# The last four weight tiles of a sublayer finished in four parts in place of three, in a two-layer decoder trunk

## What is computed

```python
mod = (cs @ ada_w[l] + ada_b[l])[:, None, :]
sh_a, sc_a, g_a, sh_m, sc_m, g_m = jnp.split(mod, N_MOD, axis=-1)
h = x * (1.0 + sc_a) + sh_a
y = gla_mixer(h, ...)    # layer 1: sb_mixer
x = layer_norm(DEEPNORM_ALPHA * x + (1.0 + g_a) * y, ln_g[l, 0], ln_b[l, 0])
h = x * (1.0 + sc_m) + sh_m
y = sq_relu_mlp(h, mlp_w1[l], mlp_b1[l], mlp_w2[l], mlp_b2[l])
x = layer_norm(DEEPNORM_ALPHA * x + (1.0 + g_m) * y, ln_g[l, 1], ln_b[l, 1])
```

## Time and profile before

| | |
|---|---|
| median of 3 runs | 2352.53 us (2351.28 to 2353.08) |
| profiled execution, its own time | 2352.33 us |
| its span | 2350.6 us |
| mean granted TensorE clock | 0.984 |
| TensorE busy | 2272.8 us, 97% of the span |
| Vector busy | 1748.5 us, 74% |
| Scalar busy | 1145.8 us, 49% |
| GpSimd busy | 25.8 us, 1% |

### The profile page before, as it was taken

How to read it: one execution, slowest core, us unless ns; L and a number is a source line. 1 busy time by engine, 2 the same in 40 slices (tenths; PEclk the granted TensorE clock), 3 DMA queues, 4 the chain that set the end, 5 groups by cost and what they waited for, 6 DMA issues and landing times.

```text
span 2350.6 us, 31199 instructions
## 1 busy us (share of the span) xinstructions
PE 2272.8 (97%) x10336; PEld 1869.3 (80%) x10336; DVE 1748.5 (74%) x1675; ACT 1145.8 (49%) x1383; POOL 25.8 (1%) x38
## 2 busy tenths in 40 slices
PE   5799999999999999999999999999999999999997
PEld 3578878778888888888878888887888888888886
DVE  6889688897777788898896865669765445556656
ACT  3254466364444545444455545545444455444443
POOL 1000000000000000000000000000000000000001
PEclk8899999999999999999999999999999999999998
DMA  9979888879888888879978865676776555655563
GB/s 381 385 299 366 326 322 310 317 278 345 332 317 329 324 336 336 335 259 343 346 298 300 309 237 179 243 273 239 277 282 217 190 183 179 212 191 196 192 229 117
DMA packets 145689, 653.91 MB, mean 278 GB/s; under 512 B 16400, under 2 KB 16656, under 8 KB 115520
## 3 DMA queue, kind: packets, MB, share of 16 engines
q1 hardware_dynamic: 144000, 642.05, 74.3%
q0 software_dynamic: 1600, 10.69, 1.2%
HBM read 650.57 MB, written 2.10 MB: 278 GB/s over the span
## 4 chain that ended last, share of the span: by engine, by line
PE 89%; DVE 5%; DMA 3%; issue 2%; ACT 0%; SPq 0%; DVEq 0%; ACTq 0%
PE ps L1090 28%; PE ps L1092 28%; PE ps L1091 28%; DMA R<-in_mods 2%; PE ps L1132 2%; DVE w_lo L696 1%; DMA mod_w<-in_mods 1%; DMA raw<-in_tiles 1%; PE ps L1145 1%; DVE X L761 1%; DVE S L760 1%; DVE mod_w L701 1%; DVE stats L763 1%; PE ps L1243 0%; PE ps L1259 0%
## 5 line engine op out<-in xcount | busy, mean ns | idle before, releaser
L696 DVE TENSOR_TENSOR w_lo<-raw,w_hi 128x1024 fp32r<-128x1024 f32 x768 | 935.5, 1224 | 541.3 <-ACT w_hi L330 512.2
L1090 PE MATMUL ps<-w_hi,h_hi 128*128 128x512 f32 x3072 | 1215.1, 396 | 4.0 <-DVE w_lo L696 4.0
L1092 PE MATMUL ps<-w_hi,h_lo 128*128 128x512 f32 x3072 | 1201.1, 391 | 0.0
L1091 PE MATMUL ps<-w_lo,h_hi 128*128 128x512 f32 x3072 | 1200.5, 391 | 0.0
L330 ACT ACTIVATE w_hi<-raw 128x1024 fp32r<-128x1024 f32 x768 | 810.1, 1059 | 749.4 <-PE ps L1092 681.9
L1090 PEld LDWEIGHTS ps<-w_hi,h_hi 128*128 128x128 f32 x3072 | 580.8, 189 | 131.3 <-DVE w_lo L696 12.9
L1092 PEld LDWEIGHTS ps<-w_hi,h_lo 128*128 128x128 f32 x3072 | 579.6, 189 | 122.8
L1091 PEld LDWEIGHTS ps<-w_lo,h_hi 128*128 128x128 f32 x3072 | 580.9, 189 | 118.2 <-issue 0.7
L701 DVE SCALAR_TENSOR_TENSOR mod_w<-mod_w,cs 128x2048 f32<-128x2048 f32 x200 | 457.1, 2286 | 14.1 <-ACT cs L453 7.7
L994 DVE TENSOR_TENSOR h_lo<-R,h_hi 128x512 fp32r<-128x512 f32 x128 | 87.8, 686 | 11.0 <-ACT h_hi L605 11.0
L367 ACT ACTIVATE S<-ps,b1t 128x256 f32<-128x256 f32 x128 | 50.3, 476 | 84.4 <-PE ps L1132 84.4
(11 more groups left out here) (155 smaller groups left out, 684.1 us busy)
## 6 DMA issues: line engine op xcount, KB each, us to landing
raw<-in_tiles SPq DMA_DIRECT2D x768, 512.0 KB, 4.3
mod_w<-in_mods SPq DMA_DIRECT2D x200, 1024.0 KB, 6.7
R<-in_mods SPq DMA_DIRECT2D x16, 1024.0 KB, 11.0
R<-in_ln_rows POOLq DMA_DIRECT2D x8, 1024.0 KB, 7.4
G<-in_mods SPq DMA_DIRECT2D x4, 1024.0 KB, 11.1
S<-in_mods SPq DMA_DIRECT2D x4, 1024.0 KB, 13.2
X<-in_x_rows SPq DMA_DIRECT2D x1, 2048.0 KB, 11.4
S<-in_b_rows POOLq DMA_DIRECT2D x2, 1024.0 KB, 7.2
```

The source lines that it names most:

```text
L696: nc.vector.tensor_tensor(w_lo[:, slot, :], raw[:, slot, :], w_hi[:, slot, :].bitcast(F32), ALU.subtract)\
L1090: mm(dst, hh, wh, start=start, stop=False, skip_group_check=more)
L1091: mm(dst, hh, wl, start=False, stop=False, skip_group_check=more)
L1092: return mm(dst, hl, wh, start=False, stop=stop, skip_group_check=more)
```

## The change

The first entry of LAST_PARTS, token group 0 with both banks, becomes two, one per bank. The waits on `part_done` count three raises per sublayer in place of two.

```diff
@@ -76,7 +76,7 @@
-LAST_PARTS = [(0, (0, 1)), (1, (0,)), (1, (1,))]
+LAST_PARTS = [(0, (0,)), (0, (1,)), (1, (0,)), (1, (1,))]
@@ -753,7 +753,7 @@
                 stage = S[:, tok * TW + ns[0] * SW:tok * TW + ns[0] * SW + width]
                 if half == 1 and (tok, ns) != LAST_PARTS[-1]:
-                    dve.wait_ge(part_done, 2 * occ + LAST_PARTS.index((tok, ns)) + 1)
+                    dve.wait_ge(part_done, (len(LAST_PARTS) - 1) * occ + LAST_PARTS.index((tok, ns)) + 1)
                 else:
                     dve.wait_ge(tile_used, HALF_END[occ][half])
```

## The result

The changed kernel takes 2358.59 us (median of 16 runs, 2354.03 to 2361.14), the one before 2353.59 (16 runs beside them, 2349.18 to 2357.59). The ratio is 1.0021, with a 95% interval of 1.0014 to 1.0027: about 5.0 us slower, 3.3 to 6.4. The forecast was 2.5 us slower, within 0.2%, in a range that ended at 2358.4. The direction was right, the size half of what came, and the time lies just outside the range.

A forecast was written before the change was run, and what follows sets the result against it. TensorE, busy 97% of the span, was taken to bound the kernel. Delays at three ends less the tail's gain, 1.34 + 1.04 + 1.08 - 0.99 = +2.5 us, on the 2352.53 median gave 2355.0, range 2352.8 to 2358.4.

The forecast's parts named there:

- Vector is 0.69 us late for the last product: Sublayer ends: Vector starts the last product 0.69 us after its bank is free; the split alone gains 0.7 us per end.
- Two more instructions of Vector: Each end: an extra product and update of half width, some 0.4 us, covered by TensorE's longer parts.
- TensorE's first part becomes too short for the fourth tile: Ends one to four: TensorE waits for tile four's low half; last product 1.34, 1.04, 1.08 us later, fourth level.
- The tail: After the fourth end: token 0's variance comes earlier, so GpSimd's train ends 0.99 us earlier; bounds 0.4 and 0.99.
- The rival of the held product: Fourth end: GpSimd holds Vector's last product, so the gain there falls to about 0.4 us; 2355.6 us, chance 18%.
- a fall as a rival of 22% for one and 12% for more: Clock falls in the first end's gaps, 1.7 us lost, 2356.7 (22%); at more than one end, 2358.4 (12%).
- these gaps are shorter than the 1.72 us that the clock has survived: Argument against clock falls at more than one end, the case of 2358.4 us, chance 12%.
- 0.19 + 3 x 0.23: Third end: TensorE's new gap, the old 0.19 us plus three matmuls; up to 1.9 us from the last matmul's start.
- The rival without stalls: TensorE's waits don't come: three ends gain 0.7 us each and the tail 1.6; 2348.8 us, chance 6%.
- three ends costing half of what is worked out: Reason given for the range's lower end, 2352.8 us: first three ends lose half the computed delays.

The follow-up runs named there:

- vector_only: Kernel before, TensorE keeping its three parts, Vector taking token group 0 in two pieces of 512 columns; ratio 1.0004 (0.9994 to 1.0013), 0.9 us slower.
- tensor_only: Kernel before with TensorE running the four parts, Vector taking token group 0 in one piece after the second; ratio 1.0032 (1.002 to 1.0045), 7.5 us slower.
- hooks_early_four: Changed kernel, Vector taking out the first half's columns after copies of tiles 3 and 7, not 8 and 12, in go and ao; ratio 1.0004 against before.
- late_and_mixed: Kernel before with Vector in four pieces, TensorE keeping six matmuls per tile at ends one to three, bank-by-bank order after tile one at the fourth; ratio 0.9999.
- four_at_end_four: Kernel before with the four parts at the fourth end only; ratio 0.9987 (0.9978 to 0.9996), 2350.68 against 2353.81 us.
- mixed_at_end_four: Kernel before with MIXED order and four Vector pieces at the fourth end only, transposes behind it left out; ratio 0.999, 2350.86 against 2352.48 us.

## Why the prediction was right or wrong

- **Vector is 0.69 us late for the last product**: right, and the four parts end it; in every profile with both halves of the change it starts the last product 0.48 to 0.49 us after the last matmul's start. I had used 0.43, which makes up most of the 0.07 to 0.08 us by which each end came out longer than worked out. Two more instructions of Vector, where nothing covers them, cost 0.5 us an end (vector_only), not 0.4.
- **TensorE's first part becomes too short for the fourth tile**: right, term by term. From the copies' ends, 1.42, 1.12, 1.15 and 0.04 us in place of 1.34, 1.04, 1.08 and -0.04 (profiles whose clock held). tensor_only shows that the loss is in TensorE's order, vector_only that it isn't in Vector's.
- **The tail**: right. 0.94 us shorter with the last product level, 0.90 us together, against 0.99. The rival of the held product fell: it took 0.69 us beside GpSimd, and the update with both inputs in SBUF was stretched to 1.76. That is as the Trainium skill (GPSIMD Engine Reference, Key points) has it, contention for instructions with two SBUF inputs or in a two-port mode.
- **The clock: the failed step.** The sum took it at nothing, and a fall as a rival of 22% for one and 12% for more. The step that failed reads "against: these gaps are shorter than the 1.72 us that the clock has survived": at the third end the clock fell after an idle stretch of 1.55 us, in two profiles of four. (That gap was also worked out wrong, as 0.19 + 3 x 0.23 = 0.88. Two tiles stand before it and each lost three matmuls: 0.19 + 6 x 0.2267 = 1.55, as measured.) At the first end, with a first pause of 2.5 to 2.7 us, it fell in all three unfilled profiles. A fall costs 1.6 to 1.7 us in the section. Three in three and two in four make some 1.65 + 0.8 = 2.5 us on average. With the 2.8 us of waiting that is 5.3, against 5.0 measured (3.3 to 6.4). Filling the gaps took the slow matmuls away in three profiles; by the runs the loss was then 2.4 us, with an interval that overlaps that of the change. That these pauses bring the clock down, and that transposes in them hold it, is thus shown by the traces; the averages rest on few profiles.
- The length of a pause doesn't decide alone. After one of 2.16 us the clock stayed up (hooks_early_four). With the order of before it fell after one of 1.96 us (late_and_mixed), and not in four other profiles with a pause of 1.67 to 2.19 us there (before, vector_only, four_at_end_four, mixed_at_end_four).
- Part of a fall at the third end may come back. In the two profiles with one (the changed kernel's first, tensor_only) the way on to the fourth end was 713.0 us, in the four profiles of the change and its filled forms without a fall there it was 714.0 to 714.2. But before, without a fall, also has 713.0, and hooks_early_four 713.2, so this can be chance. If it isn't, the sum is 4.7 in place of 5.3, which the measured 5.0 can't tell apart.
- The working had the evidence: pauses of 2.26 and 2.09 us had brought a fall, and the new pauses were worked out as 2.4. Taking the term as a rival and not as part of the sum put the likeliest case at 2.5 us where 4 to 6 was the better reading.
- **The rival without stalls**: fell. What keeps TensorE busy is an order with more matmuls in front of tile four (twelve in MIXED, where four equal parts have nine); it gained where Vector had nothing else to do, the fourth end.
- The median of the changed kernel lies some 1.1 us above what its ratio to the three first runs of before would give, since before itself measured 2353.59 in 16 runs, 2352.53 in three. The range, given in us, had no room for that, and by this the time lies just outside it. Its lower end doesn't follow from its reason either: three ends costing half of what is worked out give 1.73 - 0.99 = 0.7 us slower, 2353.3, not 2352.8.

## What to carry to other kernels

When work is cut finer so that a consumer can start sooner, look at what the coarse piece was hiding at its own front: here the first part's matmuls covered the last tile's way through two other engines, and cutting the part in half uncovered it. Cut after that point instead (the last tile's products), or only where the trace shows the consumer free, as at the end of the kernel. And count a new pause of TensorE at its length plus what the clock may take after it, or fill it with matmuls without use that end before the data comes.

## What the runs showed of the hardware

- The same pauses brought the clock to 1.2 GHz in one execution and left it in another (third end, two profiles of four). A fall costs only where TensorE would not be waiting: in late_and_mixed seven matmuls at a pitch of 0.43 us cost less than 0.1 us.
- Eighteen transposes of 128 x 128, 2.13 us of TensorE's time, stood in each pause of some 2.4 us of the first end in three profiles, and the clock fell in none.
- Runs of one kernel differ by over 8 us (before: 2349.18 to 2357.59). In the profiles 6 us stand ahead of the first end (449.8 to 456.1) and about 1 us behind the third, while a section with the same order, copies and clock repeats within 0.07 us. A change of 1 us is seen in the sections and not in the medians.
